# The last layer's end in a two-layer diffusion-transformer kernel: three experts kept on the chip in place of two, the last weight chunks cut by columns, and the final norm done half by half

## The chip, the cores and the metric

The kernel runs on one core of a Trainium2 chip. The core has a matrix engine (TensorE, PE in the profile; its weight loads are a row of their own, PEld), a vector engine (VectorE, DVE), an activation engine (ScalarE, ACT), GpSimd (POOL) and SyncE (SP), and 16 DMA engines that carry what SP's queue and POOL's queue ask for. The metric is the device time of one execution in microseconds (us); lower is better.

## What is computed

Two layers over 256 context tokens and 256 latent tokens of width 1024. The change lies in the second layer's mixture of experts and in the norm behind it:

```python
def moe(h, ...):                       # 256 latent tokens in the last layer
    ...                                # two experts of 16 for each token, weights sum to 1
    for e in range(N_EXPERTS):
        he = jax.nn.silu(h @ w_e_gate[e]) * (h @ w_e_up[e])      # 1024 -> 512, f32
        y = y + gates[:, e:e + 1] * (he @ w_e_down[e])           # 512 -> 1024
    return y
...
    x = x + ga2 * y                    # last layer: latent tokens alone
return rmsnorm(x, g_final)
```

## The kernel before

**The stream of weights.** In the last layer each expert needs four chunks of gate weights (g), four of up weights (u) and four of down weights (d), 512 KB each. SP issues them in one fixed order into a ring of 30 slots (L658 to L674); expert e's d chunks stand behind g and u of expert e+1, and the order ends with d14, g15, u15, d15. PE takes each chunk as it lands. The small number behind a letter is the expert's.

**One expert.** The tokens of an expert stand in up to 64 slots, so an output tile has 64 rows. Each f32 product is therefore made as two: the first half of the output's columns (q=0) goes to partitions 0 to 63, the second half (q=1) to partitions 64 to 127. The two use different column halves of PE's array. `into_hidden1` (L1205) makes g and u, `turn_hidden1` (L1216) transposes, `down1` (L1227) multiplies with d; DVE makes the hidden product (L2120), copies the transposed one (`hidden_copy`, L2126) and weighs the result by the layer's gate into `ytile1` (`result1`, L2134). A d chunk holds 128 rows of all 1024 columns, so each chunk of `down1` feeds one matmul for q=0 and one for q=1.

**Back to token order.** For experts 0 to 13 (`HELD = 14`) POOL stores `ytile1` to DRAM by row number (`store`, L778). When these stores have landed (L788), POOL issues four gathers of 128 rows x 4 KB (L791), two for each token tile t: the row of the token's first and of its second expert. DVE adds them to the residual with the routing weights (`gathered(t)`, two operations of L1698). The results of experts 14 and 15 stay on the chip: PE multiplies them with a matrix that puts each slot's row in its token's place, weight included (`put`, L1260, 64 rows of the array for q=0 and the other 64 for q=1), and accumulates in four banks of PSUM. That matrix is `put_back`, made from `weighed` by PE transposes (L1244) in one of the `ROWSTEPS` side steps (`last_rows`) that ride along with the experts. Step 0 of them (L1238) makes eight matmuls of 64 output rows: four on the first column half of the array, then four on the second.

**The end.** DVE adds the put-back sums to each token tile (L2232), ACT squares it (L1682) and takes the root (L1684), DVE inverts it (L2235) and scales the row (L1698, `outt`), SP sends it out (L703). Every engine works its instructions off in the order of the code. On DVE the order after the last expert's hidden copy is `gathered(0)`, `result1(15)`, `gathered(1)`, sums.

Of the kernel before, what the change touches and what calls it, by code (L numbers as in the profile page):

```python
# [15 lines left out]
P = 128  # L16
# [33 lines left out]
HELD = NE - 2  # L50
ROWSTEPS = 10
# [79 lines left out]
def build(nc, x, c, ctx_tok, c_ctx, w_ada, b_ada, g_norm1, w_in, lam_qk, g_subln, w_attn_out,  # L131
# [22 lines left out]
    cst = view("cst", [P, C_COLS], F32, place(C_COLS * 4))  # L154
# [53 lines left out]
    put_back = view("put_back", [P, 2, 2, P], F32, rQ + 28 * KB)  # L208
    weighed = view("weighed", [P, 2, 2, 2, HC], F32, rQ + 30 * KB)
# [62 lines left out]
    zss = small("zss", [P, 3, 2])  # L272
# [349 lines left out]
    def _(sp):  # L622
# [7 lines left out]
        for i in range(DEPTH):  # L630
# [26 lines left out]
            else:  # L657
                for n, (kind, e, ch) in enumerate(r_stream):  # L658
# [10 lines left out]
                    if kind == "d":  # L669
# [38 lines left out]
    def _(pool):  # L708
# [17 lines left out]
        for i in range(DEPTH):  # L726
# [47 lines left out]
            else:  # L774
# [55 lines left out]
    def _(pe):  # L830
# [201 lines left out]
        for i in range(DEPTH):  # L1032
# [199 lines left out]
            def last_rows(k):  # L1232
# [7 lines left out]
                elif k == ROWSTEPS - 1:  # L1240
                    pe.wait_ge(rt_loc, i + 1)
                    for t in range(2):
                        for j in range(2):
                            m = pe.transpose(ps[:, 7, (2 * t + j) * P:(2 * t + j + 1) * P],  # L1244
                                             weighed[:, t, j, :, :].rearrange("p c s -> p (c s)"), ident)
# [8 lines left out]
            def put(e):  # L1254

                pe.wait_ge(u_y, NE + e + 1)
                pe.wait_ge(l_c, ROWSTEPS)
                for t in range(2):
                    for q in range(2):
                        m = pe.matmul(last_bank(t)[:, q, :], put_back[HC * q:HC * (q + 1), t, e - HELD, :],  # L1260
                                      ytile1[HC * q:HC * (q + 1), e % 2, :], start=e == HELD, stop=e == NE - 1,
                                      skip_group_check=True)
                    if e == NE - 1:
                        m.then_inc(z_put, 1)
# [26 lines left out]
            else:  # L1291
                turn_pair(0)
                for e in range(NE):
                    into_hidden1("g", e)
                    if e == NE - 1:
                        put(HELD)
# [9 lines left out]
                    if e == HELD:  # L1306
                        turn_hidden1(e)
                    if 1 <= e <= HELD:
                        down1(e - 1)
                    if e == HELD:  # L1310
                        down1(e)
                turn_hidden1(NE - 1)
                down1(NE - 1)
                put(NE - 1)
            over = pe.value_load(most[0:1, 0:1], min_val=0, max_val=T)
            with pe.If(over > CAP[i]):
                if i == DEPTH - 1:
                    pe.wait_ge(l_c, ROWSTEPS)
                    pe.wait_ge(u_y, NE + NE)
# [34 lines left out]
    def _(act):  # L1354
# [171 lines left out]
        for i in range(DEPTH):  # L1526
# [127 lines left out]
            else:  # L1654
                tokens_a(0)
                for e in range(NE):
# [3 lines left out]
                    if e == 0 or 2 <= e < ROWSTEPS + 1:  # L1660
# [4 lines left out]
                        elif k == ROWSTEPS - 1:  # L1665
                            dst = put_back[:, :, :, :].rearrange("p t j n -> p (t j n)")
# [3 lines left out]
                        act.activation(dst, ps[:, 7, :], ACT.Copy).then_inc(l_c, 1)  # L1670
# [9 lines left out]
        for t in range(2):  # L1680
            act.wait_ge(z_sum, t + 1)
# [580 lines left out]
```

## Time and profile before

| | |
|---|---|
| median of 3 runs | 1519.94 us (1519.35 to 1521.89) |
| the profiled execution, its own time | 1516.55 us |
| its span, first to last instruction | 1514.7 us |
| PE / DVE / ACT busy | 91% / 53% / 44% of the span |
| mean granted PE clock | 0.952 of full speed |

The span is what the rows below are measured in: their times count from its first instruction. The time of the profiled execution is 1.9 us more than its span. The clock share tells which of its two levels (2.4 GHz at 1.00, 1.2 GHz at 0.50) the matrix engine was granted. A matmul in f32 stands in the trace as two records, so x8 means four matmuls.

### The profile page before, as it was taken

The page shows a single profiled execution, that of the slowest core. Times are in us where ns is not written, and L with a number is a line of the kernel's source. Part 1 is how long each engine was busy: PE and PEld are TensorE (multiplying, and loading weights), DVE is VectorE, ACT ScalarE, POOL GpSimd, SP SyncE. Part 2 cuts the span into 40 slices and gives each one's busy share as a digit, 9 for nine tenths or more (in the row PEclk, how much of TensorE's full clock was granted, in tenths as well). Part 3 has the DMA queues.
Part 4 walks back from the last instruction along what each step waited for, and adds up shares of the span by engine and source line. Part 5 has one row for each costly group of instructions (what it writes and reads, how often), then busy time and mean ns, then how long its engine had stood idle before and what let it go on. Part 6 is the DMA issues. An engine that isn't in the chain of part 4 may idle for free.

```text
span 1514.7 us, 21474 instructions
## 1 busy us (share of the span) xinstructions
PE 1380.5 (91%) x8076; PEld 1044.2 (69%) x8076; DVE 797.0 (53%) x1313; ACT 667.4 (44%) x1104; POOL 167.3 (11%) x188
## 2 busy tenths in 40 slices
PE   4799999999998994899999992999998897999996
PEld 2478777886556873788888872998885595655652
DVE  2412344414774616899999974567427765111113
ACT  3442122334665315588888864563246743010001
POOL 5210110001330000041111102000000000000001
PEclk8799999999998997899999996999999998999998
DMA  9673564334882233699999984355332158999996
GB/s 369 216 271 118 195 238 153 96 97 166 259 258 71 84 124 115 205 392 389 392 380 375 371 312 174 101 151 180 99 122 72 56 201 319 414 415 416 414 415 258
DMA packets 116054, 357.96 MB, mean 236 GB/s; under 512 B 13889, under 2 KB 14210, under 8 KB 115330
## 3 DMA queue, kind: packets, MB, share of 16 engines
q1 hardware_dynamic: 91232, 272.81, 48.8%
q0 software_dynamic: 23984, 81.85, 15.1%
q10 hardware_dynamic: 754, 2.15, 0.4%
q8 instruction: 57, 0.93, 0.2%
q14 instruction: 27, 0.22, 0.0%
HBM read 341.38 MB, written 25.69 MB: 242 GB/s over the span
## 4 chain that ended last, share of the span: by engine, by line
PE 84%; DMA 6%; DVE 5%; ACT 3%; issue 2%; POOL 0%; ACTq 0%; POOLq 0%; DVEq 0%
PE ps L592 19%; PE ps L594 19%; PE ps L593 19%; PE ps L1205 7%; PE ps L1227 3%; PE ps L859 3%; PE ps L983 2%; PE ps L1006 2%; PE ps L1188 2%; DMA w_raw<-in_w_ada 2%; DMA ring<-in_w_e_down 1%; PE ps L994 1%; DMA ring_h<-in_w_e_down 1%; PE ps L1145 1%; PE ps L950 1%
## 5 line engine op out<-in xcount | busy, mean ns | idle before, releaser
L588 DVE TENSOR_TENSOR w_lo<-w_raw,w_hi 128x1024 fp32r<-128x1024 f32 x224 | 270.2, 1222 | 307.2 <-ACT w_hi L584 305.7
L584 ACT ACTIVATE w_hi<-w_raw 128x1024 fp32r<-128x1024 f32 x224 | 235.6, 1058 | 317.8 <-PE ps L594 312.5
L592 PE MATMUL ps<-h_hi,w_hi 128*128 128x512 f32 (+1 forms) x704 | 248.9, 354 | 11.1 <-issue 5.7
L594 PE MATMUL ps<-h_hi,w_lo 128*128 128x512 f32 (+1 forms) x704 | 247.2, 351 | 0.0
L593 PE MATMUL ps<-h_lo,w_hi 128*128 128x512 f32 (+1 forms) x704 | 247.2, 351 | 0.0
L592 PEld LDWEIGHTS ps<-h_hi,w_hi 128*128 128x128 f32 x704 | 134.3, 191 | 33.6 <-issue 9.6
L594 PEld LDWEIGHTS ps<-h_hi,w_lo 128*128 128x128 f32 x704 | 134.1, 190 | 18.7
L593 PEld LDWEIGHTS ps<-h_lo,w_hi 128*128 128x128 f32 x704 | 134.2, 191 | 18.3
L588 DVE TENSOR_TENSOR w_lo_more<-w_raw,w_hi_more 128x1024 fp32r<-128x1024 f32 x96 | 114.9, 1222 | 4.5
L584 ACT ACTIVATE w_hi_more<-w_raw 128x1024 fp32r<-128x1024 f32 x96 | 101.2, 1060 | 22.0 <-PE ps L594 19.4
L557 POOL DMA_DIRECT2D w_raw<-in_w_ada x88 | 63.2, 727 | 350.1 <-PE ps L859 345.2
L1461 ACT ACTIVATE att_e<-ps,aneg 128x512 f32<-128x512 f32 (+1 forms) x96 | 58.2, 612 | 48.7 <-DVE aneg L1819 48.0
L1205 PE MATMUL ps<-ring,xT 128*64 128x256 f32 x560 | 65.2, 381 | 1.4 <-DMA ring<-in_w_e_up 1.4
L859 PE MATMUL ps<-w_raw,cond 128*32 128x256 f32 x704 | 52.2, 398 | 6.9 <-DMA w_raw<-in_w_ada 6.9
L1205 PEld LDWEIGHTS ps<-ring,xT 128*64 128x64 f32 x560 | 40.3, 137 | 24.9 <-issue 6.1
L1818 DVE TENSOR_REDUCE amax<-ps 128x2 f32<-128x1024 f32 (+1 forms) x48 | 50.1, 1045 | 13.6 <-PE ps L983 13.5
L592 PE MATMUL ps<-w_hi,xg_hi 128*128 128x512 f32 x128 | 52.6, 411 | 4.8 <-DVE xg_lo L2089 4.8
L1622 ACT ACTIVATE sg<-ps 128x256 f32<-128x256 f32 x16 | 6.1, 383 | 112.7 <-PE ps L1205 112.7
L983 PE MATMUL ps<-qk 64*128 64x512 f32 (+1 forms) x192 | 49.0, 590 | 6.1 <-ACT att_e L1461 4.7
L1006 PEld LDWEIGHTS ps<-v_tok,att_at 128*128 128x128 f32 x320 | 39.6, 192 | 19.2 <-issue 13.3
L1006 PE MATMUL ps<-v_tok,att_at 128*128 128x128 f32 x320 | 48.4, 290 | 3.8 <-ACT att_at L1470 2.8
L594 PE MATMUL ps<-w_hi,xg_lo 128*128 128x512 f32 x128 | 51.9, 406 | 0.0
(309 smaller groups left out, 2517.7 us busy)
## 6 DMA issues: line engine op xcount, KB each, us to landing
w_raw<-in_w_ada POOLq DMA_DIRECT2D x88, 512.0 KB, 5.5
w_raw<-in_w_e_gate SPq DMA_DIRECT2D x64, 512.0 KB
w_raw<-in_w_e_up SPq DMA_DIRECT2D x64, 512.0 KB
w_raw<-in_w_e_down SPq DMA_DIRECT2D x64, 512.0 KB
w_raw<-in_w_in SPq DMA_DIRECT2D x56, 512.0 KB
ring<-in_w_e_up SPq DMA_DIRECT2D x40, 512.0 KB, 13.4
w_raw<-in_w_gate SPq DMA_DIRECT2D x32, 512.0 KB
ring<-in_w_e_down SPq DMA_DIRECT2D x32, 512.0 KB
```

Source lines behind the costliest of these rows:

```text
L557: sp.dma_start(ada_slot(m), w_chunk(w_ada[layer], CK * ch, CW * g)).then_inc(ada_in[m if m < AF else m % AB], 16)
L584: act.activation(whi(n), raw[:, slot(n), :, :], ACT.Copy).then_inc(hi_ready, 1)
L588: dve.tensor_tensor(wlo(n), raw[:, slot(n), :, :], whi(n).bitcast(F32), ALU.subtract).then_inc(lo_ready, 1)
L592: pe.matmul(acc, sh, mh, start=first, stop=False, skip_group_check=True)
L593: pe.matmul(acc, sh, ml, start=False, stop=False, skip_group_check=True)
L594: return pe.matmul(acc, sl, mh, start=False, stop=last, skip_group_check=True)
L859: m = pe.matmul(ps[r0:r0 + AROWS, 7, 0:AC], at_g, ada_slot(m_)[:, k, half * AC:(half + 1) * AC], start=first, stop=last, skip_group_check= ...
L983: m = pe.matmul(ps[:, 2 * (j % 2) + m_, 0:keys(q)], QK[d, h, q * P:(q + 1) * P], QK[d, HEADS + h, 0:keys(q)], start=True, stop=True)
L1006: m = pe.matmul(ps[:, 6, 0:P], AT[:, t % 2, k * P:(k + 1) * P], V[:, k, h * P:(h + 1) * P], start=k == 0, stop=k == nk - 1, skip_group_che ...
L1205: m = pe.matmul(ps[HC * half:HC * (half + 1), 0 if kind == "g" else 1, 0:DE // 2], xT1[:, (e // 2) % 2, kt, HC * (e % 2):HC * (e % 2 + 1)] ...
L1461: act.activation(E[:, b, m_, 0:keys(q)], ps[:, 2 * b + m_, 0:keys(q)], ACT.Exp, bias=aneg[:, b, m_:m_ + 1], scale=ATT_SCALE, accum_out=asu ...
L1818: link(dve.tensor_reduce(amax[:, b, :], ps[:, 2 * b:2 * b + 2, 0:keys(q)], AX.X, ALU.max))
```

## The change

`HELD` becomes 13: expert 13's result is no longer stored, the gathers wait for the stores of experts 0 to 12 alone, and the put-back takes experts 13, 14 and 15. Its matrix needs one more side step (`ROWSTEPS = 11`, two more transposes and one copy on ACT). `put` is cut by q: for one expert and one q it makes the matmuls of both token tiles. Experts 13 and 14 are put back between g15 and u15. The last two d15 chunks are loaded as 256 rows x 512 columns (2 KB pieces in DRAM) in place of 128 rows x 1024 columns: the third chunk holds what q=0 still needs, the fourth what q=1 needs. DVE does both `gathered` ahead of expert 15's result, makes that result in two halves of 64 partitions, and adds the sums in four halves of 512 columns; ACT squares four halves.

```diff
-HELD = NE - 2
-ROWSTEPS = 10
+HELD = NE - 3
+ROWSTEPS = 11
...
-                    if kind == "d":
+                    if kind == "d" and e == NE - 1 and ch >= 2:
+                        src = w_e_down[i, e, 2 * P:4 * P, (ch - 2) * CW:(ch - 1) * CW].rearrange(
+                            "(k p) n -> p k n", p=P)
+                    elif kind == "d":
                         src = w_e_down[i, e, ch * P:(ch + 1) * P, :].rearrange("p (h n) -> p h n", h=2)
...
                 for j in range(2):
-                    pool.wait_ge(e_out[i][j], 16 * (HELD // 2))
-                pool.wait_ge(l_c, ROWSTEPS - 1)
+                    pool.wait_ge(e_out[i][j], 16 * ((HELD + 1 - j) // 2))
+                pool.wait_ge(l_c, ROWSTEPS - 2)
...
-            def put(e):
-
-                pe.wait_ge(u_y, NE + e + 1)
+            def put(e, q):
+                pe.wait_ge(u_y, NE + (NE + q if e == NE - 1 else NE - 1))
                 pe.wait_ge(l_c, ROWSTEPS)
                 for t in range(2):
-                    for q in range(2):
-                        m = pe.matmul(last_bank(t)[:, q, :], put_back[HC * q:HC * (q + 1), t, e - HELD, :],
-                                      ytile1[HC * q:HC * (q + 1), e % 2, :], start=e == HELD, stop=e == NE - 1,
-                                      skip_group_check=True)
-                    if e == NE - 1:
-                        m.then_inc(z_put, 1)
+                    m = pe.matmul(last_bank(t)[:, q, :], put_back[HC * q:HC * (q + 1), e - HELD, t, :],
+                                  ytile1[HC * q:HC * (q + 1), e % 2, :], start=e == HELD, stop=e == NE - 1,
+                                  skip_group_check=True)
+                if e == NE - 1 or (e == HELD and q):
+                    m.then_inc(z_put, 1)
+
+            def down_last():
+                pe.wait_ge(u_hc, NE + NE)
+                pe.wait_ge(u_y, NE + NE - 2)
+                for ch in range(4):
+                    n = r_place[("d", NE - 1, ch)]
+                    pe.wait_ge(r_in[n % RING], r_base(n) + 16 * (n // RING + 1))
+                    for j in range(2):
+                        q, kt = (j, ch) if ch < 2 else (ch - 2, 2 + j)
+                        m = pe.matmul(ps[HC * q:HC * (q + 1), 3 + (NE - 1) % 2, :],
+                                      heT1[:, (NE - 1) % 2, kt % 2, HC * (kt // 2):HC * (kt // 2 + 1)], r_slot(n)[:, j, :],
+                                      start=kt == 0, stop=kt == 3, skip_group_check=True)
+                    m.then_inc(r_used, 1)
+                    if ch == 3:
+                        put(NE - 1, 0)
...
                     into_hidden1("g", e)
                     if e == NE - 1:
-                        put(HELD)
+                        for held in (HELD, HELD + 1):
+                            for q in range(2):
+                                put(held, q)
...
                 turn_hidden1(NE - 1)
-                down1(NE - 1)
-                put(NE - 1)
+                down_last()
+                put(NE - 1, 1)
...
                 hidden_copy(NE - 1)
-                dve.wait_ge(y_in[2], 32 * DEPTH)
-                gathered(0)
-                result1(NE - 1)
-                dve.wait_ge(y_in[3], 32 * DEPTH)
-                gathered(1)
+                for t in range(2):
+                    dve.wait_ge(y_in[2 + t], 32 * DEPTH)
+                    gathered(t)
+                dve.wait_ge(z_put, 1)
+                for q in range(2):
+                    rows = slice(HC * q, HC * (q + 1))
+                    dve.wait_ge(r_used, r_done("d", NE - 1) - 1 + q)
+                    dve.tensor_tensor(ytile1[rows, 1, :], ps[rows, 4, :], ga_half[rows, :], ALU.mult).then_inc(u_y, 1)
...
-        for t in range(2):
-            z = y1L[:, t, :].rearrange("p (q n) -> p q n", q=2)
-            dve.wait_ge(z_put, t + 1)
-            dve.tensor_tensor(z, last_bank(t), z, ALU.add).then_inc(z_sum, 1)
+        for q in range(2):
+            dve.wait_ge(z_put, 2 + q)
+            for t in range(2):
+                z = y1L[:, t, q * CW:(q + 1) * CW]
+                dve.tensor_tensor(z, last_bank(t)[:, q, :], z, ALU.add).then_inc(z_sum, 1)
```

On DVE, behind the last expert's hidden copy, the order before is this (`he` and `heT` are the hidden product and its transposed copy, `ytile` the weighed result, `y_last` the gathered rows):

```order
L2120 TENSOR_TENSOR he_92<-ps,sg_91 128x256
L2126 COPY heT_93<-ps 128x256
L1698 SCALAR_TENSOR_TENSOR y_last<-y_last,gates,token_major 128x1024
L1698 SCALAR_TENSOR_TENSOR y_last<-y_last,gates 128x1024
L2134 TENSOR_TENSOR ytile_94<-ps,ga_half 128x512
L1698 SCALAR_TENSOR_TENSOR y_last<-y_last,gates,token_major 128x1024
L1698 SCALAR_TENSOR_TENSOR y_last<-y_last,gates 128x1024
```

And in the changed kernel:

```order
L2148 TENSOR_TENSOR he_92<-ps,sg_91 128x256
L2154 COPY heT_93<-ps 128x256
L1726 SCALAR_TENSOR_TENSOR y_last<-y_last,gates,token_major 128x1024
L1726 SCALAR_TENSOR_TENSOR y_last<-y_last,gates 128x1024
L1726 SCALAR_TENSOR_TENSOR y_last<-y_last,gates,token_major 128x1024
L1726 SCALAR_TENSOR_TENSOR y_last<-y_last,gates 128x1024
L2227 TENSOR_TENSOR ytile_94<-ps,ga_half 64x512 x2
```

All four additions of gathered rows now stand ahead of the last expert's result, which is two operations.

On PE, from the d chunks of experts 13 and 14 (the row with x16) to the end, before (here each row counts whole matmuls):

```order
L1227 MATMUL ps<-ring_h,heT_93 64x512 x16
L1205 MATMUL ps<-ring_g,xT_90 64x256 x16
L1260 MATMUL ps<-ytile_94,put_back 128x512 x4
L1205 MATMUL ps<-ring_g,xT_90 64x256 x8
L1205 MATMUL ps<-ring_86,xT_90 64x256 x8
L1216 MATMUL ps<-cst,he_92 128x128 x2
L1227 MATMUL ps<-ring_86,heT_93 64x512 x8
L1260 MATMUL ps<-ytile_94,put_back 128x512 x4
```

And in the changed kernel:

```order
L1231 MATMUL ps<-ring_h,heT_93 64x512 x16
L1209 MATMUL ps<-ring_g,xT_90 64x256 x16
L1263 MATMUL ps<-ytile_94,put_back 128x512 x8
L1209 MATMUL ps<-ring_g,xT_90 64x256 x8
L1209 MATMUL ps<-ring_86,xT_90 64x256 x8
L1220 MATMUL ps<-cst,he_92 128x128 x2
L1277 MATMUL ps<-ring_86,heT_93 64x512 x8
L1263 MATMUL ps<-ytile_94,put_back 128x512 x4
```

Between g15 and u15 stand eight put-back matmuls instead of four; the number behind u15 is the same.

## Rows read from the trace of the kernel before

**Rows 1.** The page: share of the span on the chain that ended last.
```profile
PE 84%; DMA 6%; DVE 5%; ACT 3%; issue 2%; POOL 0%; ACTq 0%; POOLq 0%; DVEq 0%
```

**Rows 2.** Busy time by stretch: clock, DMA share and GB/s are the last three.
```profile
5.00:10.00 5.00, 0.00 (x0) 0.00 (x0) 0.00 (x0) 1.49 (x2) 5.00 (x8) 1.00 1.03 387
1480.00:1485.00 5.00, 3.75 (x26) 1.58 (x26) 0.69 (x1) 0.00 (x0) 0.34 (x1) 1.00 1.03 419
1490.00:1493.00 3.00, 2.01 (x20) 1.11 (x18) 0.00 (x0) 0.00 (x0) 0.00 (x0) 1.00 1.02 410
1493.00:1495.00 2.00, 1.10 (x10) 0.35 (x4) 0.75 (x2) 0.00 (x0) 0.00 (x0) 1.00 0.94 379
1495.00:1497.50 2.50, 1.97 (x4) 0.33 (x4) 1.52 (x3) 0.00 (x0) 0.00 (x0) 0.53 0.85 349
```

**Rows 3.** The chain that ended last: start us, us, what.
```profile
1434.07 3.58 PE ps L1227 x16
...
1448.52 3.45 PE ps L1205 x32
...
1499.64 3.09 PE ps L1227 x8
...
1502.76 0.69 DVE ytile L2134
...
1504.68 1.30 DVE y_last L1698
...
1506.00 1.24 DVE y_last L2232
...
1507.26 1.16 ACT z_sq L1682 x2
...
1508.44 0.30 ACT zss L1684
...
1510.36 1.28 DVE outt L1698
```

**Rows 4.** Timeline of POOL: start us, us, instruction, idle time before it.
```profile
1465.03 0.97 POOL L778 DMA_INDIRECT yhalf<-ytile,row_of  x1 [14.00 <-DVE ytile L2134]
1477.94 0.97 POOL L778 DMA_INDIRECT yhalf<-ytile,row_of  x1 [11.95 <-DVE ytile L2134]
1484.66 0.99 POOL L791 DMA_INDIRECT y_last<-yhalf,loc  x1 [5.74 <-issue]
```

**Rows 5.** DMA queues (packets, MB, share) in 1476:1486, then two in 1488:1498.
```profile
q0 software_dynamic: 80, 0.18, 4.5%
...
q0 software_dynamic: 552, 2.02, 49.7%
q1 hardware_dynamic: 488, 1.75, 43.2%
```

**Rows 6.** Timeline of PE, 1484 to 1500.
```profile
1485.85 1.08 PE L1205 MATMUL ps<-ring_g,xT 128*64 128x256 f32 x8 [0.15 <-issue]
1486.86 1.99 PE L1260 MATMUL ps<-ytile,put_back 64*128 64x512 f32 x8
1488.78 1.95 PE L1205 MATMUL ps<-ring_g,xT 128*64 128x256 f32 x16
...
1492.58 1.08 PE L1205 MATMUL ps<-ring,xT 128*64 128x256 f32 x8 [0.99 <-DMA ring<-in_w_e_up]
...
1495.18 1.97 PE L1227 MATMUL ps<-ring,heT 128*64 128x512 f32 x4 [0.55 <-DVE heT L2126]
```

**Rows 7.** L1238, its records: duration ns min/median/max, first and last start.
```profile
L1238 PE MATMUL ps<-cst,mod x16: 272/273/322, 1286.5 to 1287.8; 128*64 128x128 f32 x16
```
**Rows 8.** L1238 alone in its first 0.47 us: length, PE busy (records), clock, DMA.
```profile
1286.50:1286.97 0.47, 0.43 (x4) 1.00 1.14 366
```

**Rows 9.** Timeline of PE and DVE: a full-array f32 product; the first gathered addition.
```profile
80.30 3.94 PE L950 MATMUL ps<-cst,f_feat 128*128 128x256 f32 x17
...
1496.04 1.28 DVE L1698 SCALAR_TENSOR_TENSOR y_last<-y_last,gates,token_major 128x1024 f32<-128x1024 f32 x1 [0.95 <-DMA y_last<-yhalf,loc]
```

More of the change, by code:

```diff
@@ L153, in build @@
     wlo4 = view("w_lo", [P, SPL, CK, CW], F32R, o_lo)
-    cst = view("cst", [P, C_COLS], F32, place(C_COLS * 4))
+    o_cst = place(C_COLS * 4)
+    cst = view("cst", [P, C_COLS], F32, o_cst)
     rX, rH, rQ, rV, rG = place(16 * KB), place(32 * KB), place(32 * KB), place(16 * KB), place(32 * KB)
@@ L1239, in last_rows @@
                                       start=True, stop=True, skip_group_check=True)
[L1240 removed]
+                elif k >= ROWSTEPS - 2:
                     pe.wait_ge(rt_loc, i + 1)
[L1242 to L1244 removed]
+                    j0 = 2 * (k - ROWSTEPS + 2)
+                    for j in range(j0, min(j0 + 2, NE - HELD)):
+                        for t in range(2):
+                            m = pe.transpose(ps[:, 7, (2 * (j - j0) + t) * P:(2 * (j - j0) + t + 1) * P],
                                              weighed[:, t, j, :, :].rearrange("p c s -> p (c s)"), ident)
@@ L1679, in _ @@
         warm(ACT.Sqrt)
-        for t in range(2):
-            act.wait_ge(z_sum, t + 1)
-            act.activation(zsq[:, t, :], y1L[:, t, :], ACT.Square, accum_out=zss[:, 0, t:t + 1]).then_inc(z_ss, 1)
-            act.wait_ge(z_ss, t + 1)
-            act.activation(zss[:, 1, t:t + 1], zss[:, 0, t:t + 1], ACT.Sqrt, bias=epst[:, 0:1], scale=1.0 / D).then_inc(z_std, 1)
+        for q in range(2):
+            for t in range(2):
+                part = slice(q * CW, (q + 1) * CW)
+                act.wait_ge(z_sum, 2 * q + t + 1)
+                act.activation(zsq[:, t, part], y1L[:, t, part], ACT.Square, accum_out=zss[:, q, t:t + 1]).then_inc(z_ss, 1)
+                if q == 0:
+                    act.wait_ge(z_ss, 2 * t + 1)
+                    act.activation(zss[:, 2, t:t + 1], zss[:, 0, t:t + 1], ACT.Identity, bias=epst[:, 0:1],
+                                   scale=1.0 / D).then_inc(z_ss, 1)
+                else:
+                    act.wait_ge(z_ss, 5 + t)
+                    act.activation(zss[:, 3, t:t + 1], zss[:, 1, t:t + 1], ACT.Sqrt, bias=zss[:, 2, t:t + 1],
+                                   scale=1.0 / D).then_inc(z_std, 1)
     @block.vector
@@ L2228, in _ @@
         dve.wait_ge(z_first, 2)
-        for t in range(2):
-            z = y1L[:, t, :].rearrange("p (q n) -> p q n", q=2)
-            dve.wait_ge(z_put, t + 1)
-            dve.tensor_tensor(z, last_bank(t), z, ALU.add).then_inc(z_sum, 1)
+        for q in range(2):
+            dve.wait_ge(z_put, 2 + q)
+            for t in range(2):
+                z = y1L[:, t, q * CW:(q + 1) * CW]
+                dve.tensor_tensor(z, last_bank(t)[:, q, :], z, ALU.add).then_inc(z_sum, 1)
         for t in range(2):
             dve.wait_ge(z_std, t + 1)
-            link(dve.reciprocal(zss[:, 2, t:t + 1], zss[:, 1, t:t + 1]))
-            stt(outt[:, t, :], y1L[:, t, :], zss[:, 2, t:t + 1], token_major[:, 3, :], ALU.mult, ALU.mult).then_inc(out_ready, 1)
+            link(dve.reciprocal(zss[:, 4, t:t + 1], zss[:, 3, t:t + 1]))
+            stt(outt[:, t, :], y1L[:, t, :], zss[:, 4, t:t + 1], token_major[:, 3, :], ALU.mult, ALU.mult).then_inc(out_ready, 1)
     es.close()
```

35 lines of the change are left out of this document (18 added, 17 removed).

## The prediction

> **What bounds the kernel now.** I read the chain of waits first. PE carries 84% of it [rows 1], so a change at the end can only win or lose what hangs behind the last weights. The chain's last pieces are the two last chunks of d15 on PE, the weighed result, the second `gathered` addition, the sum, the square, the root and `outt` [rows 3]. Second I read the stretches before it. The DMA engines are full (share 1.02 to 1.03, 410 to 419 GB/s) until 1493, and the rate is still 349 GB/s up to 1497.5 [rows 2]. So the end is fixed by bytes: every byte asked for before the last chunk delays it, and a byte that only changes its place does not. Third, the DMA queues. In 1488 to 1498 the POOL queue (q0) moved 2.02 MB and SP's queue (q1) 1.75 MB [rows 5]: while gathers are under way, weights come at less than half rate. Last, PE's timeline [rows 6]: the last g15 chunk starts at 1485.85, put-back at 1486.86, u15 at 1488.78, the last u15 chunk at 1492.58 after a wait for its DMA, d15 at 1495.18.
>
> **The gathers move.** The last store is issued at 1477.94 and the first gather at 1484.66, 6.7 us later [rows 4]. Without store 13 the same step starts from 1465.03, so the gathers start near 1471.8, 12.9 us earlier. They carry 4 x 128 x 4 KB = 2.10 MB. At 419 GB/s [rows 2] that is 5.0 us of all engines, now placed ahead of d14, g15, u15 and d15 rather than among u15 and d15. Store 13 (at most 0.18 MB [rows 5], 0.4 us) disappears. The last g15 chunk therefore lands 4.6 us later: 1490.45 for 1485.85. The last d15 chunk keeps its time, minus 0.4 us. That is the term that the diff does not show: the gathers' wait, which is what the change shortens, was worth little, since the first pair is summed in the wait before d15's product and the second costs one DVE block.
>
> **More put-back, in a place where PE now has no slack.** After the last g15 chunk put-back starts 1.01 us later [rows 6], at 1491.46. Four matmuls and the turn to u15 took 1.92 us (1486.86 to 1488.78). Four more follow. The price per matmul: a full-array product of 256 columns takes 3.94 / 17 = 0.23 us per record [rows 9], so 0.9 us for a lone matmul of 512 columns (four such lengths), while eight matmuls of `down1` take 3.58 us, 0.45 each [rows 3]: two run at once, on different halves of the array. `put` now issues q=0, q=0, q=1, q=1. If the halves still overlap, four more cost 1.8 us; if not, more. The nearest row is L1238, which issues one half's four matmuls and then the other half's. Its first four records take 0.43 us [rows 8], 0.11 each; sixteen one behind the other would put 1.6 us between first and last start, and one overlap at the turn 1.5 us. The trace has 1.3 [rows 7]. So the second half began about four records early, and a block of `put` is four records long. I take full overlap, 1.8 us. Strict order stays as a rival.
>
> The Trainium skill says otherwise ("TensorE: Matmul & The Clock Gate", "The mechanism"): matmuls run strictly in program order, and only weight loads are pulled ahead. By that rule sixteen records in blocks of four overlap at the three turns alone; the sum would be that of the rival "strict order" below, 1524.8, against 1522.6 by the row. The trace's L1238 speaks against it.
>
> u15 then starts at 1491.46 + 1.92 + 1.79 = 1495.2 instead of 1488.8. Its 32 records take 3.45 us [rows 3], the last chunk starts after three quarters, 1497.8. By then all u15 has landed (four chunks of 0.52 MB, 1.25 us each, lie between it and the last d15 chunk). From there to d15 it is 2.6 us as before (1492.58 to 1495.18 [rows 6]): **d15 starts at 1500.4, 5.2 us later than before.**
>
> **The column halves.** By 1500.4 nearly everything is there: before, the last two chunks together began at 1499.64 and took 3.09 us [rows 3], so the last landed by about 1501.2, now 0.4 us earlier. The third chunk's early finish for q=0 buys nothing when the fourth is already there: eight matmuls, 3.58 us plus 0.2 of drain, end at 1504.1. The 2 KB pieces cost nothing on this path either. No row of this stretch prices them; the slowest full stretch, 387 GB/s against 419 [rows 2], would make 1.05 MB 0.2 us longer, and PE reaches it only at 1502.2. Were the cover gone, it would be those 0.2 us.
>
> **DVE's new order.** `gathered(0)` and `gathered(1)` are four operations of 1.28 to 1.30 us [rows 3, 9] and now all stand between the hidden copy and the result: 1500.4 + 5.2 = 1505.6. That is 1.5 us after PE has the product. Before, the first pair lay in the wait for d15's chunks and the second ran beside put-back. Now the first pair is hidden under d15 and the second mostly is too, but not the last 1.5 us. The result is two operations of 512 elements a row. One of 128 rows takes 0.69 [rows 3]; with half the rows the bounds are 0.35 and 0.69, and I take 0.69, as a row's length sets it in all shapes here. They end at 1506.25 and 1506.95. Put-back of q=0 takes 1.99 us [rows 6] to 1508.3; of q=1, beside it, to 1509.0.
>
> **The tail.** The half sums take 0.69 each (1.24 for the whole [rows 3]); the third, which the first last square waits for, ends at 1510.4 where the first whole sum ended at 1507.24. The half square takes between 0.58 and 1.16, about 0.65 by the same saving as DVE's; the root 0.32. From the root's end to the last `outt` it was 2.90 us (1508.74 to 1511.64) and to the span's end 3.06 more. Sum: 1510.4 + 0.65 + 0.32 + 2.90 + 3.06 = 1517.3, against a span of 1514.7: **+2.6 to +2.7 us.** The extra transposes and the copy of the eleventh side step (under 0.5 us), and the wider `weighed`, fall where PE is ahead of nothing but the DMA; every us lost there comes back in its next wait for weights. The second pair of reasons to gain, a half square (0.5 us) and no second `gathered` behind the result (2.6 us), is in this sum; it is eaten by the 5.2.
>
> The change is a difference of spans; I put it on the median: 1519.94 + 2.7 = 1522.6. The profiled execution's 1516.55 is below the median by 3.4, and I assume the same distance for both kernels.
>
> **Rivals.**
> *The weights are not late.* If the gathers give way to the weights (q0 lies in gaps), g15 ends as before. d15 then starts near 1495.3, DVE is free at 1500.5, the last chunk lands near 1500.8, q=1's two matmuls follow one another (about 2.0), the result half is there at 1503.5, put-back of q=0, behind them, ends at 1504.8, the third sum at 1506.9, the span at 1513.8: -0.9 us, or 1519.0. For it: the wait that the change removes is real on DVE. Against it: in 1488 to 1498 q0 took more than q1 [rows 5]. It decides from a g15 end before about 1487.5. Chance 0.2; that it goes below -3.0 us I give 0.05.
> *Strict order on PE.* Sixteen records take 13 lengths of 0.45 instead of 8, 2.2 us more; d15's own loss hides under DVE. +4.9 us, 1524.8. Chance 0.12.
> *The clock falls.* With gathers under way a weight chunk comes every 2.6 us or so and keeps PE busy for 1.08, 0.41 of the time. Before, PE was busy 1.10 of 2.00 us and the clock stood at 0.53 in the next stretch [rows 2]. If it is at 1.2 GHz while g15 ends and puts are made, these double: up to 1.5 + 3.7 us on top, 1523.5 to 1527.5. For it: the row. Against it: from 1487 on chunks come every 1.25 us and PE is full again. Chance 0.15 for more than 1.5 us of it.
> *The halves do what they say.* q=0's finish ahead of the last chunk would be visible only if d15 started before 1497.5; that is part of the first rival.
>
> **How the numbers follow.** The forecast, d15 late by four to six us and no more, has 0.45, its own range 1521 to 1524.5; the rest (0.08) spreads. 0.2% is 3.0 us, about what a measurement of this kernel can tell from no change. The forecast lies just inside it; four tenths of its chance lie above (0.18), and with strict order (0.11), the clock (0.13) and the rest (0.03) slower gets 0.45. Faster gets 0.07, the same 0.48. The range goes from somewhat below the first rival, 1518.3, to above strict order, 1525.8, and leaves out most of the clock's upper half.
>
> **What would show it.** Right: the first gather near 1472; the last g15 chunk near 1490 with PE waits for g15 and d14 of over 1 us a chunk; no DMA wait before d15; eight put-back matmuls in 3.7 us; DVE without a pause from the hidden copy to the result. Wrong: u15 or d15 chunks waited for, which gives the first rival; a put-back block of 5.9 us, which gives strict order; a clock of 0.5 between 1488 and 1495. The steps most open are the gathers' share of the DMA and the overlap of the put-back halves.

## The result

The changed kernel takes 1523.57 us (median of 20 executions, 1519.13 to 1529.1); the kernel before, on the same chips, 1519.11 us (20 executions, 1515.94 to 1521.89). The ratio is 1.0028 [1.0019, 1.0037]: slower by 4.3 us (2.9 to 5.6; the two medians lie 4.5 apart), where +2.7 us was forecast. The ratios here and below are of fast executions; the only one left out is one of e8_one_gather, 3899.7 us. The profiled execution took 1520.62 us with a span of 1518.4 us, 3.7 us more than the span before.

The chain of waits of the changed kernel, its end (start us, us, what; [rows 3] before):

```profile
1471.49 19.64 DMA ring_g<-in_w_e_gate
...
1491.17 1.08 PE ps L1209 x8
1492.26 3.74 PE ps L1263 x16
1496.00 3.63 PE ps L1209 x32
...
1505.97 0.69 DVE ytile L2227
...
1511.50 0.62 ACT z_sq L1704 x2
...
1512.15 0.30 ACT zss L1711
```

The last DMA on it is that of g15's last chunk, which landed at 1491.13. Behind it stand only PE, DVE and ACT; before, the chain still came from a d15 chunk.

The timeline of the changed kernel, PE, POOL and DVE together, picked in order of time (start us, us, instruction, idle time before it; [rows 4, 6] before):

```profile
1472.85 0.99 POOL L795 DMA_INDIRECT y_last<-yhalf,loc  x1 [5.92 <-DMA yhalf<-ytile,row_of]
...
1479.92 1.08 PE L1231 MATMUL ps<-ring_h,heT 128*64 128x512 f32 x4 [1.30 <-DMA ring_h<-in_w_e_down]
...
1482.44 1.96 PE L1231 MATMUL ps<-ring_h,heT 128*64 128x512 f32 x4 [1.44 <-DMA ring_h<-in_w_e_down]
...
1491.17 1.08 PE L1209 MATMUL ps<-ring_g,xT 128*64 128x256 f32 x8 [0.19 <-DMA ring_g<-in_w_e_gate]
...
1492.19 3.81 PE L1263 MATMUL ps<-ytile,put_back 64*128 64x512 f32 x16
...
1495.93 1.95 PE L1209 MATMUL ps<-ring_g,xT 128*64 128x256 f32 x16
...
1501.08 3.71 PE L1277 MATMUL ps<-ring,heT 128*64 128x512 f32 x16 [0.52 <-DVE heT L2154]
...
1505.97 1.40 DVE L2227 TENSOR_TENSOR ytile<-ps,ga_half 64x512 f32<-64x512 f32 x2
...
1506.70 2.71 PE L1263 MATMUL ps<-ytile,put_back 64*128 64x512 f32 x8 [1.92 <-DVE ytile L2227]
...
1508.79 2.48 DVE L2264 TENSOR_TENSOR y_last<-ps,y_last 128x512 f32<-128x512 f32 x4 [1.42 <-PE ps L1263]
...
1512.67 1.28 DVE L1726 SCALAR_TENSOR_TENSOR outt<-y_last,zss,token_major 128x1024 f32<-128x1024 f32 x1
```

Read it from the top. The first gather goes out at 1472.85 instead of 1484.66 [rows 4]. Some 5 us later PE begins to wait for the next d14 chunks: 1.30 us before one that it works off in 1.08 us, and 1.44 before one that takes 1.96, at a clock that has fallen (0.75 in 1480 to 1485, below). The last g15 chunk starts at 1491.17 instead of 1485.85 [rows 6]. The put-back of two experts takes 3.81 us. d15 starts at 1501.08, 5.9 us later than before, and runs as one block of 16 records without a DMA wait. PE is done at 1504.8, but DVE is in its additions until 1506.0, so PE stands 1.92 us before the last put-back.

The rest is a sum of three differences against [rows 3, 6] and the same rows here. d15 starts 5.9 us later. From there to the first sum it is 7.7 us (1501.08 to 1508.79) instead of 10.8 (1495.18 to 1506.00): 3.1 us won. Only 0.4 of it lies behind the result (1505.97 to 1508.79 instead of 1502.76 to 1506.00), where no gathered addition stands any more. The other 2.7 lie ahead of it: PE makes d15's product in 3.71 us instead of 7.53 (1495.18 to 1502.71). Its weights have landed, and the clock is full; before, PE waited for d15's chunks, and the clock stood at 0.53 [rows 2] and then at 0.50 (1497.5 to 1500). From the first sum to the root's end it is 3.66 us (to 1512.45) instead of 2.74 (to 1508.74): 0.9 us lost. 5.9 - 3.1 + 0.9 = 3.7, the difference of the spans. Of the 5.9 some 0.7 was there when the last layer's experts began (their first chunk reaches PE at 1280.32 instead of 1279.61), and it is 0.9 at the last u14 chunk, ahead of the first gather (1471.34 instead of 1470.45). The 0.7 vary from execution to execution (the last section); whether the other 0.2 are the eleventh side step is not shown.

The DMA queues of the changed kernel in 1476:1486 (packets, MB, share), the stretch in which POOL's queue moved 0.18 MB before [rows 5]:

```profile
q1 hardware_dynamic: 626, 2.28, 55.7%
q0 software_dynamic: 516, 1.92, 46.8%
```

Busy time by stretch of the changed kernel (PE, PEld, DVE, ACT, POOL, then clock, DMA share, GB/s; [rows 2] before):

```profile
1480.00:1485.00 5.00, 3.06 (x10) 0.50 (x12) 0.00 (x0) 0.00 (x0) 0.00 (x0) 0.75 1.02 419
1485.00:1490.00 5.00, 3.72 (x22) 1.35 (x24) 0.69 (x1) 0.00 (x0) 0.00 (x0) 0.91 1.03 419
...
1495.00:1500.00 5.00, 4.60 (x38) 2.37 (x34) 0.35 (x1) 0.00 (x0) 0.00 (x0) 1.00 0.60 228
```

The DMA engines carry the same 419 GB/s as before, but nearly half of it is now gathered rows. PE, which was busy for 3.75 us of 1480 to 1485 [rows 2], is busy for 3.06, part of it at the lower clock. After 1495 the transfers run out (228 GB/s, and 5 GB/s in 1500 to 1505), and when d15 starts at 1501.08 all its weights are there: 3.7 us of work on PE and 5.2 us of additions on DVE are still to be done. The bound has gone from bytes to PE's and DVE's own queues.

### The profile page after: what moved, and what is told of

The parts are those of the page before. It is cut to its first block, busy times and chain, and to the rows that moved or that the text cites. A ratio compares the mean times of both kernels' runs of the same rounds, so it can differ in the third digit from the quotient of the medians.

```text
span 1518.4 us, 21507 instructions
## 1 busy us (share of the span) xinstructions
PE 1380.6 (91%) x8086; PEld 1046.2 (69%) x8086; DVE 797.9 (53%) x1316; ACT 668.7 (44%) x1111; POOL 166.1 (11%) x187
## 4 chain that ended last, share of the span: by engine, by line
PE 83%; DMA 6%; DVE 5%; ACT 3%; issue 2%; POOL 0%; ACTq 0%; DVEq 0%; POOLq 0%
PE ps L593 19%; PE ps L595 19%; PE ps L594 19%; PE ps L1209 7%; PE ps L1231 3%; PE ps L863 3%; DMA w_raw<-in_w_ada 2%; PE ps L1010 2%; PE ps L987 2%; PE ps L1192 2%; DMA ring_g<-in_w_e_gate 1%; DMA ring<-in_w_e_up 1%; PE ps L1149 1%; PE ps L998 1%; DVE amax L1846 1%
## 5 line engine op out<-in xcount | busy, mean ns | idle before, releaser
L761 POOL DMA_INDIRECT ybuf<-ytile,row_of x16 | 27.2, 1698 | 230.3 <-DVE ytile L2135 200.0
```

## The experiments

The theory: the gathers' 2.1 MB stand ahead of d14 and g15, and PE's larger put-back has no slack behind them; what the new order at the end wins back is less. The rivals: the lower clock in the starved stretch, the third held expert itself, the column halves, and the new order on DVE. All kernels are edits of the changed one, except e9 and e10, which are edits of the kernel before. One more, e2_tiny_gathers, was to move 2.1 MB less by cutting the gathers to 16 columns; there is no time for it, so the loss without any gathered bytes is not measured. e8 takes half of them away. Each ratio is against the kernel before, run in turn on the same chip. Times inside a trace are compared only after a look at where its last layer began, since that varies by up to 4.7 us from one execution to the next (the last section). In the profiled executions of e1, e4, e8 and e11 it lies within 0.4 us of the changed kernel's.

**The gathers held back (e1_late_gathers).** They wait for expert 14's result as well, and all else stays.

```diff
                 pool.wait_ge(l_c, ROWSTEPS - 2)
+                pool.wait_ge(u_y, NE + NE - 1)
```

> The changed kernel, but POOL issues the four gathers only when expert 14's result is there, near the time that they had before. If the gathers' new place is what costs (my step), the last g15 chunk is on PE near 1486 to 1487 again instead of 1491.2, d15 starts near 1497 instead of 1501.1, and the span is 1514 to 1515.5, a ratio to before of 0.9985 to 1.0005. If the extra put-back matmuls and DVE's new order cost by themselves (first rival), d15 starts no earlier than 1500 and the ratio stays at 1.002 or more. If it is the clock (second rival), the time falls only with the 0.5 stretch near 1482, which this kernel should not have either: then look at whether the last g15 chunk moved.

Measured: 0.9999 [0.9989, 1.0009]. Its timeline of POOL, PE and DVE:

```profile
1484.07 0.99 POOL L796 DMA_INDIRECT y_last<-yhalf,loc  x1 [17.09 <-DVE ytile L2163]
...
1486.40 1.08 PE L1210 MATMUL ps<-ring_g,xT 128*64 128x256 f32 x8 [0.16 <-issue]
...
1487.41 3.81 PE L1264 MATMUL ps<-ytile,put_back 64*128 64x512 f32 x16
...
1496.86 1.08 PE L1278 MATMUL ps<-ring,heT 128*64 128x512 f32 x4 [0.55 <-DVE heT L2155]
...
1498.98 1.08 PE L1278 MATMUL ps<-ring,heT 128*64 128x512 f32 x4 [1.03 <-DMA ring<-in_w_e_down]
...
1500.27 3.21 PE L1278 MATMUL ps<-ring,heT 128*64 128x512 f32 x8 [0.21 <-DMA ring<-in_w_e_down]
...
1502.31 0.68 DVE L2228 TENSOR_TENSOR ytile<-ps,ga_half 64x512 f32<-64x512 f32 x1 [0.51 <-PE ps L1278]
...
1503.51 0.69 DVE L2228 TENSOR_TENSOR ytile<-ps,ga_half 64x512 f32<-64x512 f32 x1 [0.53 <-PE ps L1278]
...
1505.50 2.48 DVE L2265 TENSOR_TENSOR y_last<-ps,y_last 128x512 f32<-128x512 f32 x4 [1.29 <-PE ps L1264]
```

One wait on POOL brings the last g15 chunk from 1491.17 back to 1486.40, 4.8 us, and the whole loss goes with it. The put-back block still takes 3.81 us, so it isn't free by itself; but now d15's weights are what PE waits for (1.03 us before the second chunk), and the block lies in front of that wait. This is also the only place where the column halves are to be seen: q=0's result is made 1.20 us ahead of q=1's.

**Half the gathered bytes (e8_one_gather).** Only the row of each token's first expert is gathered, and it is added twice with the two routing weights. The second expert's rows are therefore not read, and the output is made without them.

```diff
-                    for s, dst in enumerate((y1L, y2L)):
+                    for s, dst in enumerate((y1L,)):
...
-                stt(y1L[:, t, :], y2L[:, t, :], gates[:, 1, 2 + t:3 + t], y1L[:, t, :], ALU.mult, ALU.add).then_inc(z_first, 1)
+                stt(y1L[:, t, :], y1L[:, t, :], gates[:, 1, 2 + t:3 + t], y1L[:, t, :], ALU.mult, ALU.add).then_inc(z_first, 1)
```

> The changed kernel with two gathers instead of four: the rows of each token's second expert are not read, and the first's are added twice in their place. 1.05 MB less. If bytes ahead of g15 are the cost, the last g15 chunk is 2.5 us earlier (1488.6 on PE instead of 1491.2) and so is d15 (1498.5), and the span is near 1516, ratio to before 1.0010 to 1.0015. If the mere number of gathers or their issue costs, the shift is not 2.5 us; if PE's block alone does, the span stays.

Measured: 1.0006 [0.9995, 1.0017]. In its timeline put-back and d15 stand 2.7 us ahead of their places in the changed kernel (1492.19 and 1501.08), somewhat over half of the 4.8 us that e1 moved:

```profile
1489.48 3.81 PE L1263 MATMUL ps<-ytile,put_back 64*128 64x512 f32 x16
...
1498.38 3.70 PE L1277 MATMUL ps<-ring,heT 128*64 128x512 f32 x16 [0.52 <-DVE heT L2154]
```

So the delay of g15 goes with the gathered bytes, not with the wait's being moved as such. The ratio is below the 1.0010 to 1.0015 that was expected, but its interval holds that range.

**Two experts held, the rest of the change kept (e3_two_held).**

```diff
-HELD = NE - 3
-ROWSTEPS = 11
+HELD = NE - 2
+ROWSTEPS = 10
...
-                        for held in (HELD, HELD + 1):
+                        for held in (HELD,):
```

> The changed kernel with two experts held as before (expert 13 is stored, the gathers wait for it, four put-back matmuls between g15 and u15); column halves, half sums and DVE's order stay. If the third held expert brings the whole loss by moving the gathers and adding four matmuls, the last g15 chunk is near 1486, d15 starts near 1495.5, and the ratio to before is 0.999 to 1.001. If the column halves, DVE's order or the half sums are what costs, it stays at 1.002 or above.

Measured: 1.0005 [0.9996, 1.0013]. The gathers wait for store 13 again, so they too are late. The column halves, the halved result, the half sums and the new order on DVE cost nothing measurable together; up to 2 us would still fit the interval. The DVE order does show what it trades: the third addition waits 1.20 us for its gather (at 1504.82 in this trace), the cover that the first one had before [rows 9].

**Put-back ahead of g15 (e4_puts_ahead).** One token tile of expert 13 is put behind the first d14 chunk and the rest of experts 13 and 14 ahead of g15, where PE waits for weights.

```diff
                     m.then_inc(r_used, 1)
+                    if e == NE - 2 and ch == 0:
+                        for q in range(2):
+                            put(HELD, q, (0,))
...
-                    into_hidden1("g", e)
                     if e == NE - 1:
-                        for held in (HELD, HELD + 1):
-                            for q in range(2):
-                                put(held, q)
+                        for q in range(2):
+                            put(HELD, q, (1,))
+                        for q in range(2):
+                            put(HELD + 1, q)
+                    into_hidden1("g", e)
```

> The changed kernel with the put-back of experts 13 and 14 moved ahead of g15 (two of its matmuls already behind the first d14 chunk), where PE waits for weights. If PE's lateness behind g15 is the path (my step), about 2.2 us of the 3.7 us block go into waits: d15 starts near 1499, the span is near 1516.2, 1.5 to 2.5 us under the changed kernel's, ratio to before 1.001 to 1.002. If the path is the last weights or the DVE block alone, nothing changes (1.0028).

Measured: 1.0015 [1.0005, 1.0025]. Its timeline of PE:

```profile
1486.64 2.95 PE L1266 MATMUL ps<-ytile,put_back 64*128 64x512 f32 x12 [0.79 <-DVE ytile L2166]
...
1489.52 5.40 PE L1209 MATMUL ps<-ring_g,xT 128*64 128x256 f32 x48
...
1498.76 4.44 PE L1280 MATMUL ps<-ring,heT 128*64 128x512 f32 x16 [0.52 <-DVE heT L2158]
```

d15 starts 2.3 us earlier, and so does the end of the span (1516.1 instead of 1518.4). By the ratios half of the loss is gone, though the two intervals overlap, so that the timed gain is not shown by itself. By the traces the size of the put-back block behind a late g15 is thus a second part of the loss; it matters only because the first part has made g15 late.

**Both at once (e11_late_puts_ahead).** The edits of e1 and e4 together.

> The changed kernel with both repairs: gathers after expert 14's result, and put-back of experts 13 and 14 ahead of g15. d15 starts half a us or so earlier than with late gathers alone, but the last weight chunk, near 1501, now binds. Ratio 0.9988 to 1.0002. If PE's block were still the bound after the gathers are moved, this one is 1 us or more faster than late gathers alone (0.9999).

Measured: 1.0004 [0.9992, 1.0016], no better than e1 alone. d15 starts 0.5 us earlier than in e1 (1496.33), but nothing comes of it:

```profile
1496.33 1.97 PE L1281 MATMUL ps<-ring,heT 128*64 128x512 f32 x4 [0.56 <-DVE heT L2159]
...
1498.62 5.11 PE L1281 MATMUL ps<-ring,heT 128*64 128x512 f32 x12 [0.32 <-DMA ring<-in_w_e_down]
```

The expectation was that the last weights bind again. This trace shows only a part of that: PE waits 0.32 us for one chunk, and for the rest it works without a pause at the lower clock (0.56 in 1495 to 1500), so that it is busy until 1503.7. Late weights and the lower clock both stand there, and one trace doesn't separate them. What is shown is that PE's savings ahead of d15 bring nothing once the gathers are held back.

**The order of before on DVE (e5_dve_order).** `gathered(1)` goes behind the result's halves again.

```diff
-                for t in range(2):
-                    dve.wait_ge(y_in[2 + t], 32 * DEPTH)
-                    gathered(t)
+                dve.wait_ge(y_in[2], 32 * DEPTH)
+                gathered(0)
...
+                dve.wait_ge(y_in[3], 32 * DEPTH)
+                gathered(1)
```

> The changed kernel with DVE's order of before: the second gathered addition stands behind the last expert's result again. My sum says it gives nothing: the result comes 1.2 us earlier (near 4.7 us behind d15's start instead of 4.9 to 5.6), but 2.6 us of additions then stand ahead of the sums, which start 7.7 us behind d15's start as in the changed kernel. Ratio to before as the changed kernel's 1.0028, within 0.001. If DVE's block ahead of the result were a loss of its own, as my prediction's paragraph on it could be read, 1.2 to 1.5 us come back, ratio near 1.0018.

Measured: 1.0021 [1.0010, 1.0031], inside the interval of the changed kernel. In its timeline the result starts 3.75 us behind d15 (4.9 in the changed kernel), but the second pair then stands ahead of the sums, which start 7.84 us behind d15 (7.7 in the changed kernel):

```profile
1502.16 3.70 PE L1277 MATMUL ps<-ring,heT 128*64 128x512 f32 x16 [0.52 <-DVE heT L2154]
...
1505.91 1.41 DVE L2226 TENSOR_TENSOR ytile<-ps,ga_half 64x512 f32<-64x512 f32 x2 [1.30 <-PE ps L1277]
...
1508.68 1.28 DVE L1726 SCALAR_TENSOR_TENSOR y_last<-y_last,gates 128x1024 f32<-128x1024 f32 x1
...
1510.00 2.48 DVE L2265 TENSOR_TENSOR y_last<-ps,y_last 128x512 f32<-128x512 f32 x4
```

Once d15 is late, DVE has more to do behind the hidden copy than PE. In either order it is the same work, with one wait of 1.3 or 1.4 us for PE in it.

**Row chunks for d15 (e6_row_chunks).** The last two chunks are loaded as 128 rows again, and both result halves wait for the last chunk.

```diff
-                        q, kt = (j, ch) if ch < 2 else (ch - 2, 2 + j)
+                        q, kt = j, ch
...
-                    dve.wait_ge(r_used, r_done("d", NE - 1) - 1 + q)
+                    dve.wait_ge(r_used, r_done("d", NE - 1))
```

> The changed kernel with the last two d15 chunks loaded by rows again. Both chunks have landed when PE comes to them, so nothing changes: ratio within 0.001 of 1.0028, d15's 16 records again over 3.1 us between first and last start. If the 2 KB pieces or the serial matmuls of one half cost, it is 0.5 us or more faster.

Measured: 1.0027 [1.0014, 1.0039]. With d15 landed before PE comes to it, the chunks' shape is without effect, as was forecast.

**The clock in the starved stretch (e7_clock_fill).** Each d14 chunk is followed by two more matmuls on the same weights, into a bank that nobody reads, so that PE has less idle time there.

```diff
                     m.then_inc(r_used, 1)
+                    if e == NE - 2:
+                        for _ in range(1):
+                            for q in range(2):
+                                pe.matmul(ps[HC * q:HC * (q + 1), 7, :], heT1[:, e % 2, ch % 2, HC * (ch // 2):HC * (ch // 2 + 1)],
+                                          r_slot(n)[:, q, :], start=True, stop=True, skip_group_check=True)
```

> The changed kernel with one more pair of matmuls into an unused bank behind each d14 chunk, where PE waits 1.3 us for the next chunk; their result is overwritten. In the changed kernel's executions the granted clock lies at 0.948 to 0.951 in 14 of 20 and those take 1522 to 1529 us; the others, 0.952 to 0.954, take 1519 to 1521. If the clock falls in the starved stretch and stays low while g15 and the put-back run, the filler keeps it up: mean clock 0.952 or more in most executions, ratio to before 1.0015 to 1.002. If the spread comes from elsewhere, the ratio stays at 1.0028.

Measured: 1.0027 [1.0017, 1.0036]. Two stretches of it:

```profile
1480.00:1485.00 5.00, 3.97 (x18) 1.03 (x16) 0.03 (x1) 0.00 (x0) 0.00 (x0) 1.00 1.02 419
...
1509.00:1512.30 3.30, 3.30 (x8) 1.25 (x6) 0.36 (x1) 0.00 (x0) 0.00 (x0) 0.50 0.03 5
```

The clock is full where it had fallen to 0.75, and in the five microseconds behind as well, and the time is the same: the weights are late there, not PE. Nor is it one execution's luck: the mean granted clock is 0.952 or more in nine of its twelve executions, against six of twenty of the changed kernel, and the ratio is unchanged. The theory that the clock fall at 1482 is part of the loss fell. The second row shows another one, in the profiled execution of this kernel and not in that of the changed one: the clock fell in the last wait, and the last put-back took 4.15 us instead of 2.71. The profiled execution of e6 has the same (its last two rows here, PE and the sums behind it):

```profile
1509.99 4.40 PE L1260 MATMUL ps<-ytile,put_back 64*128 64x512 f32 x8 [1.97 <-DVE ytile L2224]
...
1513.05 2.66 DVE L2261 TENSOR_TENSOR y_last<-ps,y_last 128x512 f32<-128x512 f32 x4 [2.40 <-PE ps L1260]
```

**The last wait filled (e12_tail_fill).** Four matmuls into a bank that nobody reads then, between d15's product and the last put-back.

```diff
                     if ch == 3:
+                        for _ in range(2):
+                            for q in range(2):
+                                pe.matmul(ps[HC * q:HC * (q + 1), 0, :], heT1[:, 1, 1, 0:HC], r_slot(n)[:, q, :],
+                                          start=True, stop=True, skip_group_check=True)
                         put(NE - 1, 0)
```

> The changed kernel with four matmuls into an unused bank between d15's product and the last put-back, where PE waits 1.9 us for DVE. In two of the four profiled kernels of this form the clock was at 0.5 just there, and the time from the result to the first sum was 3.8 and 4.4 us instead of 2.8. If that is the difference between 3.0 us of profile and 4.3 us of median, the filler brings 0.5 to 1.5 us: ratio 1.0018 to 1.0025, and no low stretch before the sums. If not, 1.0028 or more.

Measured: 1.0021 [1.0009, 1.0032]. In its timeline PE's last wait is 0.20 us, and put-back is at full clock:

```profile
1509.00 1.94 PE L1284 MATMUL ps<-ring,heT 128*64 128x512 f32 x8
...
1511.13 2.71 PE L1263 MATMUL ps<-ytile,put_back 64*128 64x512 f32 x8 [0.20 <-DVE ytile L2231]
```

The ratio lies 0.0007 below the changed kernel's, about 1 us, but the intervals overlap. This doesn't prove that the clock in the last wait costs the time that the profiled execution doesn't show; it only doesn't speak against it.

**Only the halved tail, in the kernel before (e10_half_tail).** Sums and squares by halves, without any other part of the change.

```diff
-        for t in range(2):
-            z = y1L[:, t, :].rearrange("p (q n) -> p q n", q=2)
-            dve.wait_ge(z_put, t + 1)
-            dve.tensor_tensor(z, last_bank(t), z, ALU.add).then_inc(z_sum, 1)
+        for q in range(2):
+            for t in range(2):
+                dve.wait_ge(z_put, t + 1)
+                z = y1L[:, t, q * CW:(q + 1) * CW]
+                dve.tensor_tensor(z, last_bank(t)[:, q, :], z, ALU.add).then_inc(z_sum, 1)
```

> The kernel before with only the tail of the change: four half sums, four half squares with the extra step on ACT between them. In the changed kernel each half square with its read and small step takes 0.94 us on ACT, and the third started 0.8 us after its sum was there. So the halves by themselves lose about 0.9 us: first outt near 0.9 us later, ratio 1.0003 to 1.0009. If half sums gain, as their smaller first step suggests, the ratio is under 1.

Measured: 1.0007 [0.9994, 1.0020]. The timeline of ACT and DVE:

```profile
1506.84 2.48 DVE L2241 TENSOR_TENSOR y_last<-ps,y_last 128x512 f32<-128x512 f32 x4
...
1507.57 0.63 ACT L1684 ACTIVATE z_sq<-y_last 128x512 f32<-128x512 f32 x1 [17.68 <-DVE y_last L2241]
1508.10 0.19 ACT L1684 ACTIVATION_READ_ACCUMULATOR z_sq<-y_last 128x1 f32 x1
1508.32 0.30 ACT L1687 ACTIVATE zss<-zss,epst 128x1 f32<-128x1 f32 x1
1508.52 0.61 ACT L1684 ACTIVATE z_sq<-y_last 128x512 f32<-128x512 f32 x1
...
1510.20 0.29 ACT L1691 ACTIVATE zss<-zss 128x1 f32<-128x1 f32 x1
```

Each half costs ACT 0.94 us from square to square: 0.6 for the square, 0.2 for reading the accumulator, and a small step. DVE delivers a half sum every 0.62 us, so ACT is the bound, and the third square, the first that lets a row go on, starts two steps behind the first square. From the first sum to the root's end it is 3.65 us (1506.84 to 1510.49) instead of 2.74 [rows 3]. The 0.9 us are in the trace; the ratio, whose interval holds both 0 and 0.9 us, can't show them.

**Both pairs first, in the kernel before (e9_gathered_first).** The new DVE order without anything else.

```diff
                 gathered(0)
-                result1(NE - 1)
                 dve.wait_ge(y_in[3], 32 * DEPTH)
                 gathered(1)
+                result1(NE - 1)
```

> The kernel before with one edit: both gathered additions stand ahead of the last expert's result on DVE. The second pair of gathers has landed near 1499.3, so its addition is done near 1502, before the product (1502.7). The first token tile's put-back is complete at 1504.6, the first sum ends at 1505.9 instead of 1507.2: 1.4 us less, ratio 0.9988 to 0.9996. If the additions collide with the result (landing later than 1500), nothing or a loss up to 1 us.

Measured: 0.9993 [0.9981, 1.0005], 1516.98 us. Of all the versions it has the lowest ratio, but the interval holds 1, so it isn't shown to beat the kernel before. Its timeline:

```profile
1500.57 1.29 DVE L1698 SCALAR_TENSOR_TENSOR y_last<-y_last,gates,token_major 128x1024 f32<-128x1024 f32 x1 [0.95 <-DMA y_last<-yhalf,loc]
...
1503.31 0.69 DVE L2134 TENSOR_TENSOR ytile<-ps,ga_half 128x512 f32<-128x512 f32 x1
...
1505.30 2.35 DVE L2232 TENSOR_TENSOR y_last<-ps,y_last 128x1024 f32<-128x1024 f32 x2 [1.30 <-PE ps L1260]
```

With the gathers where they were, the second pair fits into the wait for d15's last chunks, and the sums follow put-back directly. From d15's start to the first sum it is 8.8 us (1496.48 to 1505.30) instead of 10.8. Not all of that is the order: here d15 ran at the full clock,

```profile
1495.00:1500.00 5.00, 2.59 (x10) 0.62 (x10) 3.42 (x4) 0.00 (x0) 0.00 (x0) 1.00 0.76 310
```

while in the profiled execution of the kernel before it did not [rows 2]. The product is there 6.8 us behind d15's start (1503.26) instead of 7.5, so 0.7 to 0.8 of the 2.0 us are the clock and about 1.2 the order; 1.4 were expected.

## Why the prediction was right, point by point

**The gathers move: right, and the cause.** The forecast put the first gather near 1471.8 and g15's last chunk at 1490.45; the trace has 1472.85 and 1491.17, 1.1 and 0.7 us later, of which 0.7 is the later start of the whole layer. The forecast had g15's last chunk 4.6 us later than before, 5.0 for the gathers less 0.4 for store 13; the traces have 5.3, and 4.6 without the 0.7. Between e1 and the changed kernel, which both do without store 13, it is 4.8 for the 5.0, and with half the bytes 2.7 come back (e8). The sign "waits of over 1 us a chunk" holds for three waits (1.30, 1.44, 1.07) and not for the others.

**Put-back: right.** Eight matmuls were to take 3.7 us, their sixteen records took 3.81. Strict order, 5.9 us, is refuted, and with it, for PE, the sentence of the kernel's description that every engine works its instructions off in the order of the code: one half's eight records would take 3.6 us by the forecast's price, so in 3.81 us the two halves must have run beside each other from the start, although q=1's matmuls stand behind q=0's. The forecast took this from L1238, which uses the column halves of the array (128*64 in its row), while put-back uses the row halves (64*128); that the one would carry over to the other was assumed, and it did. The rule of the Trainium skill that was weighed there ("TensorE: Matmul & The Clock Gate", "The mechanism": matmuls run strictly in program order) would have given 5.9; this trace disagrees with 3.81, in e1 and e8 too. e4 and e11 show that the block's length counts only behind a late g15.

**d15 at 1500.4, no DMA wait: right.** 1501.08 less the 0.7 is 1500.4. The rival in which the weights are not late would have needed the order of e1 in the DMA; it was refuted by the queues' rows (1.92 MB of gathers in 1476 to 1486) and by PE's waits.

**Column halves: right** (e6), for the reason given: they are worth something only where d15 is waited for, as in e1.

**DVE's order: right.** The result started 4.9 us behind d15, 5.2 forecast. The half on 64 partitions took the full 0.69 to 0.70 us, the upper bound that was chosen. That the order gains nothing once d15 is late is shown by e5.

**The tail: a term mis-sized.** "The half square takes ... about 0.65" counted the square alone and let it start with its sum. ACT needs 0.94 us for each half and lags, the third square starting 0.8 us behind the end of the third sum. From the first sum to the root's end the forecast has 3.1 us (1508.3 to 1511.4), the trace 3.7: 0.6 too little. On the other side four half sums took 0.62 each instead of 0.69. What was missing is ACT's own queue of small steps, and not only a size: against the 2.74 us of before the forecast's tail is 0.3 us longer, and the traces' is 0.9 longer, in e10 without the rest of the change as well.

**The sum.** +2.7 forecast; 3.7 in the profiles, less 0.7 of a later start, gives 3.0. There is some luck in how near that is: both the forecast and this difference start from an execution of the kernel before whose d15 ran at the lower clock, and compare it with a d15 at the full one. In e9, with the same weights at the full clock, d15's product took 0.7 to 0.8 us less; against such an execution the change would lose 3.7 to 3.8 us, an estimate from the two traces. The timed difference is 4.3 (2.9 to 5.6). What lies between 3.0 and 4.3 may be nothing (3.0 is inside the interval), or that clock in d15 before, or executions of the changed kernel in which the clock falls in the last wait, which adds 1.4 to 1.7 us to the last put-back (e6, e7), or later starts of the last layer. e12 leaves this open, and how often each happens is not known from one trace a kernel. The clock rival as it was written (a low clock while g15 ends and put-back runs) did not happen in the profile of the changed kernel: 0.91 in 1485 to 1490, 1.00 behind it, a put-back of 3.81 us. In the profile of e6 the clock was 0.62 in 1490 to 1495, where g15 ended, but put-back still took 3.81 us. That the clock ahead of it isn't the loss is shown by e7.

## What to carry to other kernels

When the DMA engines are full, a wait that is shortened ahead of a transfer moves that transfer's bytes in front of others: ask which weights they now stand ahead of, and who needs those first, before counting the wait as won. A transfer that is needed late should be held back until the earlier weights are issued, even if its source is ready (here one more wait on POOL was worth about 4 us). Before an operation at the end is halved, add up the next engine's whole step for each half, small instructions included; if that step is longer than the half it waits for, halving loses.

## What the runs showed of the hardware

- Matmuls on 64 rows of the array each, on its two row halves, overlap also when the program issues blocks of one half after blocks of the other: sixteen records in 3.81 us, 0.24 each, while one record takes 0.59 (median of L1263's in the changed kernel).
- A DVE product on 64 partitions x 512 takes the same 0.69 us as one on 128 partitions x 512.
- Gathers and weight loads share the DMA engines nearly evenly by bytes while both are pending (1.92 and 2.28 MB in 10 us).
- The first expert chunk of the last layer reaches PE at 1279.6 to 1281.2 us in nine profiled executions and at 1282.4 to 1284.3 in four, those of e3, e6, e7 and e12. That is why these have late times beside ratios that are not. All four are edits of the changed kernel, and the three traces of the kernel before and its edits start early; with one trace each that may be chance, and the reason for the late start is not shown.
- After a wait of about 2 us behind d15 the clock was at full speed in some executions (last put-back 2.71 us) and at half in others (4.15 and 4.40 us), with the same instructions in the same order.
